# Fifteen slots for fetched expert rows, and one dot product in six on GpSimd and ScalarE, from the eighth top-k block on

## The chip, the cores and the metric

The kernel runs on one core of one Trainium2 chip. The metric is the device time of one execution in microseconds (us). The kernel before took 4034.56 us, the median of 3 runs (4030.64 to 4038.61).

## The reference, cut to what matters

One layer of a decoder trunk on 1024 tokens of width 1024: token mixers (a convolution and a stick-breaking attention), a cross-attention into 256 memory tokens, and then PEER, the retrieval of single-neuron experts, in which the change lies:

```
q = (h @ w_pq).reshape(b, s, 8, 2, 128)
sc = einsum('bshpc,pnc->bshpn', q, sub_keys)        # 128 keys on either side
top_v, top_i = top_k(sc, 16)
cand = top_v[..., 0, :, None] + top_v[..., 1, None, :]
best_v, best_i = top_k(cand, 16)
expert = i1 * 128 + i2                              # one of 16384
gate = softmax(best_v)
a = einsum('bthkd,btd->bthk', u_emb[expert], h)     # 16 experts of each of 8 heads
out = einsum('bthk,bthkd->btd', gelu(a) * gate, v_emb[expert])
```

The change concerns `a`, the dot products of the fetched rows of `u_emb` with the token's own `h`.

## The kernel before, in words

The kernel has four phases, one after the other: the mixers, the merge, `retrieve_phase` (L1406) and `spread_value_phase`. The tokens are treated in two halves of 512. For the first half (the "picked" half, 4 tiles of 128 tokens) the chosen experts' rows are fetched one by one and multiplied with `h` on the vector engine; for the second half (the "dense" half) TensorE multiplies `h` with all 16384 rows of `u_emb`, in 128 expert tiles.

**Top-k blocks.** `body(b)` (L2224) of the vector engine's program (DVE) finds the 16 best experts of one head for one half: `b` from 0 to 15, blocks 0 to 7 for the picked half and 8 to 15 for the dense one. It is a hand-written order of MAX8, FIND_INDEX8 and MATCH_REPLACE8 instructions and small table arithmetic. Between its steps stand `some(i)`, a sixteenth of the block's dot products each (`dots`, L2187), and `beside(b, at)` (L2200), which forms the low parts of weight tiles (`split_low`, L1380) for TensorE. There are 512 dot products, 8 heads x 4 token tiles x 16 experts, numbered `d`; `dots_before(b)` (L1512) shares them evenly over blocks 1 to 15, so that block 7 begins at d = 204.

**A dot product** (L2193) is one SCALAR_TENSOR_TENSOR on 128 partitions x 1024 elements. It reads the fetched rows in `slots[s]` and `h_rows[:, t]`, both in SBUF, writes the product back into the slot and sums it into `tables.coef`. It raises `dotted`.

**The fetches.** `fetch(d)` (L1575) is an indirect DMA issued by GpSimd (POOL): 128 rows of 4 KB, one for each partition, into slot `d % 7`. It waits until the dot product seven before it is done (`dotted`). The fetches are POOL's only work from the end of the cross-attention's output projection on; during that projection it also makes the low parts of eight weight tiles (`give_low`, L1585), three ahead of the first fetch and five between fetches.

**TensorE** (PE) runs `product` (L1385), 24 matmuls of 128x128 by 512 columns for each weight tile: high by high, high by low and low by high. The order of the tiles is fixed by `tile_order` (L1278): about nine expert tiles and the next head's two query tiles for each block. `hhi[0]` and `hlo[0]` are the high and low parts of the first half's `h`; their last reader is the tile ("query", 7, 1), whose place is after the third expert tile of block 6. **ScalarE** (ACT) makes a tile's high part (`split_high`, L1376), copies or gelus a product out of its PSUM bank (`query`, `expert`, L1922) and copies scores. The weights are loaded by the sync engine's queue (SP), one tile whenever the product four before it is done.

At the end of the phase ACT waits for all dot products and applies gelu to `coef` (L1950).

Of the kernel before, what the change touches and what calls it, by code (L numbers as in the profile page):

```python
# [14 lines left out]
P = 128  # L15
D = 1024
# [9 lines left out]
PH = 8  # L26
# [5 lines left out]
GT = 4  # L32
# [5 lines left out]
F32 = mybir.dt.float32  # L38
# [5 lines left out]
ALU = mybir.AluOpType  # L44
ACT = mybir.ActivationFunctionType
# [77 lines left out]
class SumSquares:  # L123
# [22 lines left out]
    def sum(self, nc, pe, ones):  # L146
        pe.wait_ge(self.added, NC)
        for h in range(2):
            mm = nc.tensor.matmul(self.out[:, h], ones, self.total[:, h * H:h * H + H], start=True, stop=True)
        mm.then_inc(self.done, 1)  # L150
# [1105 lines left out]
BLOCKS = 2 * PH  # L1256
# [1 line left out]
PICKED, DENSE = slice(0, TD), slice(TD, T)  # L1258
SIDE = (PICKED, DENSE)
EXPERT_LOADS = 4  # L1260
ROWS_SLOTS = 7
GELU_SLOTS = 5


# [141 lines left out]
def retrieve_phase(nc, carry, front, front_at, wide_at, room_at, weights, memory, tables, x_in, w_cross, w_query, u_stream, x_out, x2t, keysT, ffn_gain,  # L1406
# [8 lines left out]
    with Phase(nc, "ret") as m:  # L1415
# [28 lines left out]
        x_rows = [m.at(f"x_rows{t}", [P, D], F32, room_at + x * KB) for t, x in enumerate((83, 87, 91, 0))]  # L1444
        h_rows = m.at("h_rows", [P, GT, D], F32, room_at + 24 * KB)
        slots = [m.at(f"urow{s}", [P, D], F32, room_at + x * KB) for s, x in enumerate((53, 57, 61, 65, 69, 73, 0))]
        keys = m.at("keys", [P, 2, KEYS], F32, front_at + 4 * 8192)
        asked = [[xT[:, 3 + 2 * i + c, PICKED] for c in range(2)] for i in range(2)]
        bent_out = [xT[:, 3 + i, DENSE] for i in range(GELU_SLOTS)]
# [49 lines left out]
        gate_made = m.sem("gate_made", start=1)  # L1499
        held, slot_held = m.sem("held"), m.sem("slot_held")  # L1500
        rows_made = m.sem("rows_made")
        row_loaded = [m.sem(f"row_loaded{s}") for s in range(ROWS_SLOTS)]
        dotted = m.sem("dotted", start=ROWS_SLOTS)
        gelu_stored = [m.sem(f"gelu_stored{s}") for s in range(GELU_SLOTS)]
        turn_done, part_high, part_low = m.sem("turn_done"), m.sem("part_high"), m.sem("part_low")
        bent, coef_made = m.sem("bent"), m.sem("coef_made")
# [5 lines left out]
        def dots_before(b):  # L1512

            return DOTS * max(b - 1, 0) // (BLOCKS - 1)

        STARTS = [ORDER.index(("give", 1, 0)), ORDER.index(("give", 1, 2))] + [ORDER.index(("expert", 1, expert_at(b)))
                                                                                for b in range(FIRST_DENSE, BLOCKS)] + [len(ORDER) - 2]
# [47 lines left out]
        @block.gpsimd  # L1565
        def _(pool):
            nc.gpsimd.affine_select(out=ident[:], in_=ones[:], pattern=[[-1, P]], compare_op=ALU.is_equal, fill=0.0,
                                    base=0, channel_multiplier=1).then_inc(made, 1)
            for n, tile in enumerate(ORDER):
                if tiles.maker[n] and tile[:2] != ("give", 1):  # L1570
                    tiles.split_low(pool, nc.gpsimd, n)
            pool.wait_ge(h2_made, NC)
            nc.gpsimd.iota(place_at[:], pattern=[[KEYS, K]], base=0, channel_multiplier=0).then_inc(made, 1)
            nc.gpsimd.iota(fifteen[:].rearrange("p t k -> p (t k)"), pattern=[[0, ND * K]], base=K - 1, channel_multiplier=0).then_inc(made, 1)
            def fetch(d):  # L1575
                hd, k, s = d // (GT * K), d % (GT * K), d % ROWS_SLOTS
                t, j = k % GT, k // GT
                if k == 0:
                    pool.wait_ge(rows_made, hd + 1)
                pool.wait_ge(dotted, d + 1)  # L1580
                pool.sem_inc(slot_held, 1)
                nc.gpsimd.indirect_dma_start(slots[s][:], None, u_rows,  # L1582
                                             bass.IndirectOffsetOnAxis(tables.rows[:, t, hd * K + j:hd * K + j + 1], 0)).then_inc(row_loaded[s], 16)

            def give_low(k):  # L1585

                tiles.split_low(pool, nc.gpsimd, ORDER.index(("give", 1, k)))

            for k in range(3):
                give_low(k)  # L1590
            tile = ("weigh", 1, NC - 1)
            pool.wait_ge(banks.filled(tile), banks.turn(tile))
            pool.wait_ge(x2t_stored, 16 * GT)
            for d in range(DOTS):
                fetch(d)
                if d >= ROWS_SLOTS - 1 and (d - ROWS_SLOTS + 1) % 3 == 0 and (d - ROWS_SLOTS + 1) // 3 + 3 < NC:
                    give_low((d - ROWS_SLOTS + 1) // 3 + 3)

        @block.tensor
        def _(pe):  # L1600
# [162 lines left out]
        def _(act):  # L1763
# [117 lines left out]
            def query(b, c):  # L1881
                tile = ("query", b, c)
                act.wait_ge(banks.filled(tile), banks.turn(tile))
                if b >= 2:
                    act.wait_ge(scored, 2 * b - 2)
                nc.scalar.activation(asked[b % 2][c], banks.at(tile), ACT.Copy).then_inc(banks.emptied(tile), 1)
                ahead(tile)

            def copy_scores(b):
                for c in range(2):  # L1890
                    act.wait_ge(scored, 2 * b + c + 1)
                    act.wait_ge(index16, b * NU + 1)
                    if b == 0:
                        act.wait_ge(x2t_stored, 16 * GT)
                    nc.scalar.activation(sc[:, c], scps[:, c], ACT.Copy).then_inc(sc_made, 1)

            def exponent(b):
                act.wait_ge(shift_made, b + 1)
                nc.scalar.activation(expv[:], shifted[:], ACT.Exp).then_inc(exp_taken, 1)
# [22 lines left out]
            def expert(e):  # L1922
                tile = ("expert", 1, e)
                act.wait_ge(banks.filled(tile), banks.turn(tile))
                if e >= GELU_SLOTS:
                    act.wait_ge(gelu_stored[e % GELU_SLOTS], 16 * (e // GELU_SLOTS))
                nc.scalar.activation(bent_out[e % GELU_SLOTS], banks.at(tile), ACT.Gelu_apprx_tanh).then_inc(banks.emptied(tile), 1)
                ahead(tile)

            for b in range(FIRST_DENSE, BLOCKS):  # L1930
                for i, e in enumerate(experts_of(b)):
                    expert(e)
                    if i == 1:
                        exponent(b - 1)
                    if i == QUERY_BEHIND and b + 1 < BLOCKS:
                        for c in range(2):
                            query(b + 1, c)
                    if i == SCORES_BEHIND and b + 1 < BLOCKS:
                        copy_scores(b + 1)
            exponent(BLOCKS - 1)  # L1940

            def parts_high(r):
# [3 lines left out]

            for r in range(3):
                parts_high(r)
            act.wait_ge(dotted, DOTS + ROWS_SLOTS)
            nc.scalar.activation(tables.coef[:], tables.coef[:], ACT.Gelu_apprx_tanh).then_inc(bent, 1)  # L1950

        @block.vector
        def _(dve):
# [233 lines left out]
            def dots(d0, d1):  # L2187

                for d in range(d0, d1):
                    hd, k, s = d // (GT * K), d % (GT * K), d % ROWS_SLOTS  # L2190
                    t, j = k % GT, k // GT
                    dve.wait_ge(row_loaded[s], d // ROWS_SLOTS * 16 + 16)
                    nc.vector.scalar_tensor_tensor(out=slots[s][:], in0=slots[s][:], scalar=1.0, in1=h_rows[:, t], op0=ALU.mult, op1=ALU.mult,  # L2193
                                                   accum_out=tables.coef[:, t, hd * K + j:hd * K + j + 1]).then_inc(dotted, 1)

# [548 lines left out]
```

## Time and profile before

| | |
|---|---|
| median of 3 runs | 4034.56 us (4030.64 to 4038.61) |
| the profiled execution | 4050.63 us, its span 4048.8 us |
| granted TensorE clock, mean | 0.914 |
| busy | PE 3394.2, DVE 3201.9, POOL 1888.9, ACT 1457.9 us |
| top-k blocks 0 to 15 | 1661 to 2814 us of the span |
| of these, blocks 7 to 15 | 2158 to 2814 us |

Times in the trace count from the start of the span. A row of a group of instructions gives the busy time in all and the mean ns of one, and behind the bar how long the engine stood idle before them and what ended that. A row of the timeline gives start and duration in us; neighbouring instructions on one engine overlap by some 0.07 us in it, so that the distance of two starts is what an instruction costs in a full row. Where xN stands at its end, the row holds N instructions.

### The profile page before, as it was taken

What the parts mean: (1) busy time and instruction counts of PE and PEld (TensorE: products, weight loads), DVE (VectorE), ACT (ScalarE), POOL (GpSimd) and SP (SyncE); (2) the same over time, 40 slices, a digit from 0 to 9 for tenths busy, and PEclk for the clock granted to TensorE, in tenths of its full rate; (3) what the DMA queues carried; (4) which work ended last, traced back from release to release, by engine and by line L of the source; (5) the groups of instructions that cost most, each with busy time, mean ns of one, the idle gap of its engine ahead of it and who ended that gap; (6) DMA issues with size and microseconds to landing.
All of it is one profiled execution on the core that took longest, in us unless ns stands there. A gap on an engine that the chain in (4) does not pass through costs nothing. (4 is left out here: it accounts for less than half of the span.)

```text
span 4048.8 us, 46819 instructions
## 1 busy us (share of the span) xinstructions
PE 3394.2 (84%) x15298; PEld 2673.5 (66%) x15298; DVE 3201.9 (79%) x5528; ACT 1457.9 (36%) x2400; POOL 1888.9 (47%) x1508
## 2 busy tenths in 40 slices
PE   6999999998899998868989989897333788898886
PEld 5766676766577886646777777775333567677664
DVE  5677776777753513699999999998999798898988
ACT  3465555656542433222322322322222222222222
POOL 2433444333222131345556665554555466666664
PEclk9999999998999999979999999998555799999998
DMA  2111111111343322479999999997988999999997
GB/s 85 47 49 51 53 37 53 44 51 53 121 181 125 120 73 95 156 248 353 357 353 354 370 357 354 344 362 289 362 323 334 332 392 396 396 399 397 395 383 283
DMA packets 300338, 964.44 MB, mean 238 GB/s; under 512 B 30656, under 2 KB 63680, under 8 KB 297024
## 3 DMA queue, kind: packets, MB, share of 16 engines
q0 software_dynamic: 147456, 536.94, 35.3%
q1 hardware_dynamic: 150336, 390.95, 26.6%
q10 hardware_dynamic: 2304, 33.56, 2.1%
q8 instruction: 124, 2.03, 0.2%
q14 instruction: 118, 0.97, 0.1%
HBM read 861.18 MB, written 100.14 MB: 237 GB/s over the span
## 5 line engine op out<-in xcount | busy, mean ns | idle before, releaser
L2446 POOL DMA_INDIRECT spread_vrow<-in_v_rows,shared_pick_rows x512 | 712.5, 1392 | 464.9 <-DVE spread_y L2474 339.8
L1582 POOL DMA_INDIRECT ret_urow<-in_u_rows,shared_pick_rows x512 | 630.0, 1230 | 493.0 <-DVE ret_urow L2193 358.5
L2474 DVE SCALAR_TENSOR_TENSOR spread_y<-spread_vrow,shared_pick_coef,spread_y 128x1024 f32<-128x1024 f32 x512 | 639.3, 1279 | 10.1 <-DMA spread_vrow<-in_v_rows,shared_pick_rows 10.0
L2193 DVE SCALAR_TENSOR_TENSOR ret_urow<-ret_urow,ret_h_rows 128x1024 f32<-128x1024 f32 x512 | 609.8, 1227 | 28.7 <-DMA ret_urow<-in_u_rows,shared_pick_rows 26.5
L157 PE MATMUL shared_carry<-ret_hhi,shared_w_hi 128*128 128x512 f32 x1152 | 475.1, 412 | 108.6 <-DVE shared_w_lo L1382 66.1
L157 PE MATMUL spread_banks<-spread_ahi,spread_vhi 128*128 128x512 f32 x1024 | 418.8, 409 | 121.0 <-DVE spread_alo L2487 121.0
L157 PE MATMUL shared_carry<-shared_wide_hi,shared_w_hi 128*128 128x512 f32 x1152 | 459.1, 399 | 28.9 <-DVE shared_wide_lo L585 11.2
L158 PE MATMUL shared_carry<-ret_hlo,shared_w_hi 128*128 128x512 f32 x1152 | 466.0, 405 | 0.0
L158 PE MATMUL shared_carry<-shared_wide_lo,shared_w_hi 128*128 128x512 f32 x1152 | 454.8, 395 | 0.0
L159 PE MATMUL shared_carry<-shared_wide_hi,shared_w_lo 128*128 128x512 f32 x1152 | 454.2, 394 | 0.0
L158 PE MATMUL spread_banks<-spread_alo,spread_vhi 128*128 128x512 f32 x1024 | 412.1, 402 | 0.0
L159 PE MATMUL spread_banks<-spread_ahi,spread_vlo 128*128 128x512 f32 x1024 | 410.9, 401 | 0.0
L190 POOL TENSOR_TENSOR shared_w_lo<-shared_w_raw,shared_w_hi 128x1024 fp32r<-128x1024 f32 x78 | 203.5, 2611 | 390.2 <-ACT shared_w_hi L186 390.2
L157 PEld LDWEIGHTS shared_carry<-ret_hhi,shared_w_hi 128*128 128x128 f32 x1152 | 227.5, 197 | 173.3 <-issue 121.9
L636 DVE SCALAR_TENSOR_TENSOR shared_front<-mix_u,mix_cwj,shared_front 128x1024 f32<-128x1024 f32 x240 | 329.0, 1371 | 6.2 <-DVE mix_u L607 3.2
L157 PEld LDWEIGHTS spread_banks<-spread_ahi,spread_vhi 128*128 128x128 f32 x1024 | 200.4, 196 | 180.7 <-DVE spread_alo L2487 116.1
L159 PE MATMUL shared_carry<-ret_hhi,ret_wlow 128*128 128x512 f32 x768 | 311.8, 406 | 0.0
L159 PE MATMUL shared_carry<-ret_hhi,shared_w_lo 128*128 128x512 f32 x768 | 308.3, 401 | 0.0
L2582 PE MATMUL spread_banks<-spread_gate,spread_one 128*128 128x128 f16 x1024 | 113.9, 311 | 210.7 <-DVE spread_gate L2504 210.7
L2613 ACT ACTIVATE spread_ahi<-spread_act 128x512 fp32r<-128x512 f32 x128 | 81.0, 632 | 573.3 <-DVE spread_act L2483 573.3
L157 PEld LDWEIGHTS shared_carry<-shared_wide_hi,shared_w_hi 128*128 128x128 f32 x1152 | 219.7, 191 | 82.1 <-issue 28.2
L158 PEld LDWEIGHTS shared_carry<-ret_hlo,shared_w_hi 128*128 128x128 f32 x1152 | 228.0, 198 | 47.8 <-issue 1.0
(295 smaller groups left out, 6764.6 us busy)
## 6 DMA issues: line engine op xcount, KB each, us to landing
spread_vraw<-in_peer_v SPq DMA_DIRECT2D x128, 512.0 KB, 13.8
shared_w_raw<-in_peer_u SPq DMA_DIRECT2D x65, 512.0 KB, 7.1
gelu_u<-shared_front SPq DMA_DIRECT2D x128, 256.0 KB, 8.3
gates<-spread_stage ACTq DMA_DIRECT2D x16, 2048.0 KB, 9.6
spread_act<-gelu_u SPq DMA_DIRECT2D x128, 256.0 KB, 11.9
spread_graw<-gates SPq DMA_DIRECT2D x16, 2048.0 KB, 23.3
ret_wraw<-in_peer_u SPq DMA_DIRECT2D x63, 512.0 KB, 7.2
shared_w_raw<-in_w_mix SPq DMA_DIRECT2D x56, 512.0 KB, 3.4
```

The costliest lines, as they stand in the source:

```text
L157: nc.tensor.matmul(out, whi, xhi, start=(first and i == 0), stop=False)
L158: nc.tensor.matmul(out, whi, xlo, start=False, stop=False)
L159: mm = nc.tensor.matmul(out, wlo, xhi, start=False, stop=(last and i == len(terms) - 1))
L190: self.nc.gpsimd.tensor_tensor(self.lo[:, slot], self.raw[:, slot], self.hi[:, slot].bitcast(F32), ALU.subtract).then_inc(self.lo_made, 1)
L636: nc.vector.scalar_tensor_tensor(out=ybuf[:, par], in0=u[:, par, t:t + T], scalar=cwj[:, par, t:t + 1], in1=ybuf[:, par], op0=ALU.mult, op ...
L1582: nc.gpsimd.indirect_dma_start(slots[s][:], None, u_rows, bass.IndirectOffsetOnAxis(tables.rows[:, t, hd * K + j:hd * K + j + 1], 0)).then ...
L2193: nc.vector.scalar_tensor_tensor(out=slots[s][:], in0=slots[s][:], scalar=1.0, in1=h_rows[:, t], op0=ALU.mult, op1=ALU.mult, accum_out=tab ...
L2446: nc.gpsimd.indirect_dma_start(v_slots[s][:], None, v_rows, bass.IndirectOffsetOnAxis(tables.rows[:, t, j:j + 1], 0)).then_inc(row_loaded[ ...
L2474: nc.vector.scalar_tensor_tensor(out=y[:, t], in0=v_slots[s][:], scalar=tables.coef[:, t, j:j + 1], in1=y[:, t], op0=ALU.mult, op1=ALU.add ...
L2582: mm = nc.tensor.matmul(ps[:, bank, x], one1[:, b, t], gate[b][:, i, t], start=(i == 0), stop=(i == 1))
L2613: nc.scalar.activation(ahi[g % 2][:, e], act[:, e], ACT.Copy).then_inc(ahi_made, 1)
```

## The change

From dot 204 on (block 7, the eighth) the fetched rows go into fifteen slots: the seven of before and eight in the place of `hhi[0]` and `hlo[0]`. Before the fetch of dot 204 POOL waits for the tile ("query", 7, 1). Of the dots from 204 on each with d % 6 == 5 is no longer computed by DVE: POOL multiplies the slot with `h_rows` in place (TENSOR_TENSOR), behind the fetch six further on, and ACT sums the product by an ACTIVATE Copy with an accumulated output. `due` (of the ACT program) places these sums after the expert and query tiles, in proportion to the place of the tile in its block. Each fetch waits for whoever read its slot last, DVE or ACT.

```
@@ -1258,7 +1258,7 @@
-ROWS_SLOTS = 7
+ROWS_SLOTS, MORE_SLOTS = 7, 15
@@ -1444,6 +1444,7 @@
         slots = [m.at(f"urow{s}", [P, D], F32, room_at + x * KB) for s, x in enumerate((53, 57, 61, 65, 69, 73, 0))]
+        slots += [m.at(f"urow{ROWS_SLOTS + s}", [P, D], F32, wide_at + x * KB) for s, x in enumerate((0, 4, 8, 12, 32, 36, 40, 44))]
@@ -1499,8 +1500,8 @@
-        row_loaded = [m.sem(f"row_loaded{s}") for s in range(ROWS_SLOTS)]
-        dotted = m.sem("dotted", start=ROWS_SLOTS)
+        row_loaded = [m.sem(f"row_loaded{s}") for s in range(MORE_SLOTS)]
+        dotted, pool_dotted, pool_summed = m.sem("dotted"), m.sem("pool_dotted"), m.sem("pool_summed")
@@ -1512,6 +1513,17 @@
         def dots_before(b):
 
             return DOTS * max(b - 1, 0) // (BLOCKS - 1)
+
+        FIRST_POOLED, POOL_BEHIND = dots_before(PH - 1), 6
+        pooled = [d >= FIRST_POOLED and d % 6 == 5 for d in range(DOTS)]
+        slot_of = [d % ROWS_SLOTS if d < FIRST_POOLED else (d - FIRST_POOLED) % MORE_SLOTS for d in range(DOTS)]
+        held_by, landed, latest = [], [], {}
+        for d in range(DOTS):
+            user, loads = latest.get(slot_of[d], (None, 0))
+            held_by.append(user)
+            landed.append(16 * loads + 16)
+            latest[slot_of[d]] = d, loads + 1
+        upto = {kind: [sum(p is kind for p in pooled[:d]) for d in range(DOTS + 1)] for kind in (True, False)}
@@ -1573,12 +1585,17 @@
             def fetch(d):
-                hd, k, s = d // (GT * K), d % (GT * K), d % ROWS_SLOTS
+                hd, k, s = d // (GT * K), d % (GT * K), slot_of[d]
                 t, j = k % GT, k // GT
                 if k == 0:
                     pool.wait_ge(rows_made, hd + 1)
-                pool.wait_ge(dotted, d + 1)
-                pool.sem_inc(slot_held, 1)
+                if d == FIRST_POOLED:
+                    tile = ("query", PH - 1, 1)
+                    pool.wait_ge(banks.filled(tile), banks.turn(tile))
+                last = held_by[d]
+                if last is not None:
+                    pool.wait_ge(pool_summed if pooled[last] else dotted, upto[pooled[last]][last + 1])
+                    pool.sem_inc(slot_held, 1)
                 nc.gpsimd.indirect_dma_start(slots[s][:], None, u_rows,
                                              bass.IndirectOffsetOnAxis(tables.rows[:, t, hd * K + j:hd * K + j + 1], 0)).then_inc(row_loaded[s], 16)
 
@@ -1591,10 +1608,20 @@
             tile = ("weigh", 1, NC - 1)
             pool.wait_ge(banks.filled(tile), banks.turn(tile))
             pool.wait_ge(x2t_stored, 16 * GT)
+            def product(d):
+                s, t = slot_of[d], d % (GT * K) % GT
+                pool.wait_ge(row_loaded[s], landed[d])
+                nc.gpsimd.tensor_tensor(slots[s][:], slots[s][:], h_rows[:, t], ALU.mult).then_inc(pool_dotted, 1)
+
             for d in range(DOTS):
                 fetch(d)
+                if d >= POOL_BEHIND and pooled[d - POOL_BEHIND]:
+                    product(d - POOL_BEHIND)
                 if d >= ROWS_SLOTS - 1 and (d - ROWS_SLOTS + 1) % 3 == 0 and (d - ROWS_SLOTS + 1) // 3 + 3 < NC:
                     give_low((d - ROWS_SLOTS + 1) // 3 + 3)
+            for d in range(DOTS - POOL_BEHIND, DOTS):
+                if pooled[d]:
+                    product(d)
 
         @block.tensor
         def _(pe):
@@ -1927,16 +1954,39 @@
                 nc.scalar.activation(bent_out[e % GELU_SLOTS], banks.at(tile), ACT.Gelu_apprx_tanh).then_inc(banks.emptied(tile), 1)
                 ahead(tile)
 
+            summed_to = [0]
+
+            def sums(upto_dot):
+
+                for d in range(summed_to[0], max(upto_dot, summed_to[0])):
+                    if pooled[d]:
+                        hd, k, s = d // (GT * K), d % (GT * K), slot_of[d]
+                        t, j = k % GT, k // GT
+                        act.wait_ge(pool_dotted, upto[True][d + 1])
+                        nc.scalar.activation(slots[s][:], slots[s][:], ACT.Copy,
+                                             accum_out=tables.coef[:, t, hd * K + j:hd * K + j + 1]).then_inc(pool_summed, 1)
+                summed_to[0] = max(upto_dot, summed_to[0])
+
+            def due(tile):
+
+                n = tiles.place[tile]
+                b = max(b for b in range(FIRST_DENSE, BLOCKS) if STARTS[b] <= n)
+                first, after = dots_before(b), dots_before(b + 1)
+                return min(after, first + (after - first) * (n - STARTS[b]) // (STARTS[b + 1] - STARTS[b]))
+
             for b in range(FIRST_DENSE, BLOCKS):
                 for i, e in enumerate(experts_of(b)):
                     expert(e)
+                    sums(due(("expert", 1, e)))
                     if i == 1:
                         exponent(b - 1)
                     if i == QUERY_BEHIND and b + 1 < BLOCKS:
                         for c in range(2):
                             query(b + 1, c)
+                            sums(due(("query", b + 1, c)))
                     if i == SCORES_BEHIND and b + 1 < BLOCKS:
                         copy_scores(b + 1)
+            sums(DOTS)
             exponent(BLOCKS - 1)
 
             def parts_high(r):
@@ -1946,7 +1996,8 @@
 
             for r in range(3):
                 parts_high(r)
-            act.wait_ge(dotted, DOTS + ROWS_SLOTS)
+            act.wait_ge(dotted, upto[False][DOTS])
+            act.wait_ge(pool_summed, upto[True][DOTS])
             nc.scalar.activation(tables.coef[:], tables.coef[:], ACT.Gelu_apprx_tanh).then_inc(bent, 1)
 
         @block.vector
@@ -2187,9 +2238,11 @@
             def dots(d0, d1):
 
                 for d in range(d0, d1):
-                    hd, k, s = d // (GT * K), d % (GT * K), d % ROWS_SLOTS
+                    if pooled[d]:
+                        continue
+                    hd, k, s = d // (GT * K), d % (GT * K), slot_of[d]
                     t, j = k % GT, k // GT
-                    dve.wait_ge(row_loaded[s], d // ROWS_SLOTS * 16 + 16)
+                    dve.wait_ge(row_loaded[s], landed[d])
                     nc.vector.scalar_tensor_tensor(out=slots[s][:], in0=slots[s][:], scalar=1.0, in1=h_rows[:, t], op0=ALU.mult, op1=ALU.mult,
                                                    accum_out=tables.coef[:, t, hd * K + j:hd * K + j + 1]).then_inc(dotted, 1)
 
```

## Rows read from the trace of the kernel before

**Rows 1.** The page: GB/s in 40 equal slices of the span.

```profile
GB/s 85 47 49 51 53 37 53 44 51 53 121 181 125 120 73 95 156 248 353 357 353 354 370 357 354 344 362 289 362 323 334 332 392 396 396 399 397 395 383 283
```

**Rows 2.** Busy time by stretch: block 7, and blocks 7 to 15.

```profile
2158.40:2229.81 71.41, 66.68 (x286) 54.23 (x285) 70.81 (x201) 21.54 (x28) 46.07 (x36) 0.95 0.97 360
...
2158.40:2814.50 656.10, 586.13 (x2479) 475.55 (x2478) 636.39 (x1795) 190.69 (x238) 383.02 (x304) 0.94 0.96 355
```

The columns are the stretch, its length, then busy us and instructions of PE, PEld, DVE, ACT and POOL, the granted clock, the DMA share and GB/s.

**Rows 3.** Waits in blocks 7 to 15: who waited for whom, us, times, longest.

```profile
DVE ret_urow L2193 <- DMA ret_urow<-in_u_rows,shared_pick_rows: 12.7, 17, 2.0
...
PE shared_carry L157 <- DVE ret_wlow L1382: 42.6, 17, 5.2
...
POOL ret_urow L1582 <- DVE ret_urow L2193: 193.7, 85, 5.6
```

**Rows 4.** Groups of DVE instructions in blocks 7 to 14 (2158.40 to 2744.14).

```profile
L2193 DVE SCALAR_TENSOR_TENSOR ret_urow<-ret_urow,ret_h_rows 128x1024 f32<-128x1024 f32 x273 | 322.2, 1217 | 12.7 <-DMA ret_urow<-in_u_rows,shared_pick_rows 11.5
L1382 DVE TENSOR_TENSOR shared_w_lo<-ret_wraw,shared_w_hi 128x1024 fp32r<-128x1024 f32 x44 | 53.9, 1225 | 0.0
L1382 DVE TENSOR_TENSOR ret_wlow<-shared_w_raw,shared_w_lo 128x1024 fp32r<-128x1024 f32 x23 | 28.0, 1219 | 1.6 <-ACT shared_w_lo L1378 1.6
L1382 DVE TENSOR_TENSOR ret_wlow<-shared_w_raw,shared_w_hi 128x1024 fp32r<-128x1024 f32 x22 | 26.9, 1223 | 0.2 <-ACT shared_w_hi L1378 0.2
```

**Rows 5.** Timeline of DVE where block 7 begins.

```profile
2155.26 1.22 DVE L2193 SCALAR_TENSOR_TENSOR ret_urow<-ret_urow,ret_h_rows 128x1024 f32<-128x1024 f32 x1
...
2162.28 1.22 DVE L2193 SCALAR_TENSOR_TENSOR ret_urow<-ret_urow,ret_h_rows 128x1024 f32<-128x1024 f32 x1
...
2163.42 1.22 DVE L2193 SCALAR_TENSOR_TENSOR ret_urow<-ret_urow,ret_h_rows 128x1024 f32<-128x1024 f32 x1
```

**Rows 6.** Timeline of POOL in block 1: its elementwise instructions between fetches.

```profile
1693.80 2.35 POOL L1382 TENSOR_TENSOR ret_wlow<-shared_w_raw,shared_w_lo 128x1024 fp32r<-128x1024 f32 x1
...
1700.59 2.40 POOL L1382 TENSOR_TENSOR shared_w_lo<-ret_wraw,shared_w_hi 128x1024 fp32r<-128x1024 f32 x1
...
1707.42 2.38 POOL L1382 TENSOR_TENSOR shared_w_lo<-ret_wraw,shared_w_hi 128x1024 fp32r<-128x1024 f32 x1
...
1716.41 2.35 POOL L1382 TENSOR_TENSOR ret_wlow<-shared_w_raw,shared_w_hi 128x1024 fp32r<-128x1024 f32 x1
...
1723.49 2.60 POOL L1382 TENSOR_TENSOR ret_wlow<-shared_w_raw,shared_w_lo 128x1024 fp32r<-128x1024 f32 x1
```

**Rows 7.** Timeline of DVE beside them.

```profile
1694.80 0.28 DVE L2099 MATCH_REPLACE8 ret_sc<-ret_top,ret_sc 128x128 f32<-128x128 f32 x1
1695.22 2.03 DVE L2193 SCALAR_TENSOR_TENSOR ret_urow<-ret_urow,ret_h_rows 128x1024 f32<-128x1024 f32 x1
...
1698.93 0.68 DVE L2028 TENSOR_TENSOR shared_front<-shared_front,ret_sq 128x512 f32<-128x512 f32 x1
...
1701.08 3.00 DVE L2193 SCALAR_TENSOR_TENSOR ret_urow<-ret_urow,ret_h_rows 128x1024 f32<-128x1024 f32 x1
...
1707.26 3.63 DVE L2193 SCALAR_TENSOR_TENSOR ret_urow<-ret_urow,ret_h_rows 128x1024 f32<-128x1024 f32 x1
...
1715.51 3.48 DVE L2111 TENSOR_TENSOR ret_cand<-ret_top 128x64 f32<-128x64 f32 x4
...
1724.35 2.29 DVE L2028 TENSOR_TENSOR shared_front<-shared_front,ret_sq 128x512 f32<-128x512 f32 x1
...
2183.11 0.62 DVE L2111 TENSOR_TENSOR ret_cand<-ret_top 128x64 f32<-128x64 f32 x4
```

**Rows 8.** POOL's fetches: blocks 7 to 14 as a group, and landings of blocks 7 to 15.

```profile
L1582 POOL DMA_INDIRECT ret_urow<-in_u_rows,shared_pick_rows x275 | 350.0, 1273 | 238.3 <-DVE ret_urow L2193 174.6 <-issue 63.7
...
DMA to landing us min/median/max: 4.4/8.2/12.9
```

**Rows 9.** Timeline of POOL: one fetch of the slow form.

```profile
2156.45 1.99 POOL L1582 DMA_INDIRECT ret_urow<-in_u_rows,shared_pick_rows  x1 [0.30 <-issue]
```

**Rows 10.** ACT instructions of L2648: a sum over 1024 elements, as the change adds.

```profile
L2648 ACT ACTIVATE spread_vrow<-spread_y x4: 1040/1040/1057, 4013.6 to 4016.7; 128x1024 f32<-128x1024 f32 x4
```

## The prediction

> **What bounds the kernel now.** I read the stretches by block first, because the change touches only blocks 7 to 15. There DVE is busy for 636.4 of 656.1 us, 97%, and in block 7 for 70.8 of 71.4 us, while POOL is busy for 383 us, ACT for 191 us and PE for 586 us [rows 2]. The waits come next. DVE waits 12.7 us for fetched rows in the whole stretch, PE waits for low parts that DVE makes (42.6 us for one of the two tiles alone), and POOL waits 193.7 us for DVE to release slots [rows 3]. So everybody waits for DVE, and DVE for almost nobody. The end of the stretch is set by the sum of DVE's instructions; deeper slots have 12.7 us to gain, and only time taken off DVE has more. The DMA share of 0.96 at 355 GB/s [rows 2] looks like a second bound, to which I come below.
>
> **The dots taken from DVE.** Dots 209, 215, ..., 509 go, which is (509 - 209)/6 + 1 = 51 of the 308 from 204 on. In a full row a dot costs the distance of two starts, 1.14 us [rows 5]. That is 51 x 1.14 = 58.1 us off DVE.
>
> **What the product on POOL costs DVE.** The kernel before already has such a meeting: in block 1 POOL runs five elementwise instructions of 128x1024 of 2.35 to 2.60 us between fetches, while DVE runs the same dots [rows 6, 7]. Put beside each other:
> - POOL from 1693.80 to 1696.15. DVE's MATCH_REPLACE8 at 1694.80 takes its usual 0.28 us; the dot that starts at 1695.22 takes 2.03 us, not 1.22: 0.81 us more, and ends 1.10 us after POOL does.
> - POOL from 1700.59 to 1702.99. The dot at 1701.08 takes 3.00 us: 1.78 more. Again it ends 1.09 us after POOL.
> - POOL from 1707.42 to 1709.80. The dot at 1707.26 takes 3.63 us: 2.41 more, POOL's whole duration.
> - POOL at 1716.41: the four small additions of L2111 take 3.48 us where they take 0.62 elsewhere, 2.86 more. POOL at 1723.49: an addition of L2028 takes 2.29 us, not 0.68, 1.61 more.
>
> The dots are not slowed, they stand still until POOL is through. The mean of the five is (0.81 + 1.78 + 2.41 + 2.86 + 1.61)/5 = 1.89 us. The size depends on what DVE has at hand: instructions with two operands in SBUF stop, the searches with one go on. Dots and low parts, at 1.14 us each, fill (273 + 44 + 23 + 22) x 1.14 = 413 of the 585.7 us of blocks 7 to 14 [rows 4], so at least 71% of DVE's time is of the kind that stops. 0.71 x 2.39 = 1.70 us is then a lower estimate and the full 2.39 us an upper one. I take 1.89, the measured mean of the nearest rows, which lies between: 51 x 1.89 = 96.4 us on DVE. The ends for the range are the mean of the three smallest, (0.81 + 1.61 + 1.78)/3 = 1.40, and the full 2.39 us: 71 and 122 us.
>
> The Trainium skill has a rule on this (SBUF — State Buffer, section "SBUF: two separate sides"): the port pair that VectorE and GpSimd share is an exclusive lock for a whole instruction, and a VectorE instruction with two SBUF inputs needs it against a GpSimd instruction that reads SBUF. Applied without a discount for one-input work it charges the whole of each product, 51 x 2.39 = 122 us, which would put the result at about 4092; the rows say that a part falls on searches that go on.
>
> **The slots.** Up to 12.7 us of DVE's waits for rows [rows 3] can go. A row lands 8.2 us after its issue at the median and 12.9 at most [rows 8]; a dot passes every 656.1/308 = 2.13 us [rows 2], so seven slots cover 15 us less the issue and fifteen cover 32. I take 11 us off; the ends are 0 and 12.7. The change of slots costs once: dot 204 goes into slot 0, where 203 was, not 197, so its fetch can only start when dot 203 is done. In the trace that is at 2156.4, and dot 204 starts at 2162.28, 5.9 us on [rows 5]. The fetch takes about 1.3 us on POOL and 8.2 us to land [rows 8], 9.5 in all, so DVE waits 3.6 us; I take 4, between 0 and 8. The wait for the tile ("query", 7, 1) costs nothing: that tile stands behind the third expert tile of block 6, and block 6 is over when dot 204 is due.
>
> **POOL.** It issues as many fetches as before, 34.1 a block at 1273 ns + 0.30 us of issue [rows 8, 9], 53.7 us, and 5.7 products of 2.39 us plus up to 0.6 us for the DVE instruction in flight, 17 us. The sum is 71 us in a block of now some 77; it fits, with 6 us to spare. Behind a product only fetches are queued, and fifteen slots hide a delay of 3 us.
>
> **ACT.** 51 sums of 1.04 us [rows 10], some 55 to 65 us with the reading of the sum, beside 191 us in 656 [rows 2]. It stands behind the making of the next high part, in time in which ACT waits for PE, so I cost it at nothing; if that cover went, it would be at most about 1.2 us for each. ACT waits for POOL there, with its gelus and high parts queued behind. The product is asked for when dot d - 9 is done, nine dots or 19 us ahead of DVE's own place, and ACT asks at about DVE's place; it finds it done. PE waits for DVE already; it waits more.
>
> **The sum.** -58.1 + 96.4 - 11 + 4 = +31 us. Against the profiled execution, 4050.6 becomes 4082; it lies 16 us above the median of the runs, so for the median 4034.6 + 31 = 4066 us. What a measurement can tell here from no change is 0.2%, 8 us.
>
> **The rivals.**
> - *POOL and DVE run beside each other* (faster). If the products fell on searches, or a multiplication did not stop the dots, the change would be worth -58.1 - 11 + 4 = -65 us, about 3970. A part of that comes with a share of overlap: it decides where the mean stop per product is under (58.1 + 7 - 8)/51 = 1.12 us. Only one of the five meetings is below that [rows 7]: 8%. The DMA engines would not forbid it: the stretch would need 355 x 656/591 = 394 GB/s, and slices of the next phase reach 396 to 399 [rows 1]. The same page of the Trainium skill gives some 358 GB/s as the limit between HBM and one core, by which the DMA would hold this rival at no gain at all; the trace disagrees, by those slices.
> - *The stop and the saving cancel* (same): a mean stop of about 1.3 us, if the products follow the release of a slot by DVE and so tend to meet the table work. 51 x 1.3 = 66, -58 - 7: +1 us, about 4036. 5%.
> - *POOL becomes the bound* (slower still). A fetch takes 1.99 us where a DVE instruction has just begun [rows 9], and behind a product DVE always has one waiting. If the mean rose from 1.27 to 1.7 us, a block would take POOL 34.1 x 2.0 + 17 = 85 us against 77, 8 more in each of nine blocks: +31 + 72, about 4137. It decides from a mean of 1.45 us on. Against it: 1273 ns is the mean under the same crowd of dots. 5%.
> - *The whole product stops DVE* (2.39 us each and no wait saved): 122 - 58 + 4 = +68, 4102; the upper end of the forecast, not a case of its own.
>
> **How the numbers follow.** The forecast, DVE bound with a stop of 1.4 to 2.4 us, has 82%: its own range goes from 71 - 58 - 12.7 + 4 = +4, which is 4039, to 4102. The range of 8 in 10 leaves out the gain, POOL as the bound and the very ends: 4042 to 4094. Faster by over 0.2%: 8%. Within 0.2%: the 5% and a sliver of the forecast's lower end, 6%. Slower: 86%.
>
> **What the changed profile would show.** Right: dots of L2193 beside a POOL TENSOR_TENSOR of 2 to 3.6 us, 51 of them or nearly, and a mean of that group of up to 1.22 + 96/257 = 1.6 us, less what falls on other instructions; the blocks from 7 on at 76 to 78 us instead of 73; DVE waits for rows of a few us, one of 4 us at the start of block 7; POOL's products at 2.4 to 3.4 us; PE's waits for low parts up by about 30 us. Wrong: dots that stay at 1.22 us beside the products; ACT waiting for POOL with PE behind it; POOL without idle time. The forecast falls if the mean stop is under 1.3 us, or if DVE has idle time again in the stretch.

## The result, and the profile after

The changed kernel takes 4076.5 us (median of 4 runs, 4071.9 to 4080.5), the kernel before 4036.6 us (4 runs beside it): a ratio of 1.010, 95% interval 1.0081 to 1.0118. It is 40 us slower; the forecast was 31. Beside the experiments the kernel before took 4033 to 4035 us (medians of 17 to 23 runs); by these the loss is 41 to 44 us. The profiled execution took 4071.9 us, its span 4070.2 us.

Busy time by stretch in the changed kernel, columns as in [rows 2]: block 7, and blocks 7 to 15.

```profile
2146.99:2226.15 79.16, 67.55 (x285) 54.69 (x284) 75.18 (x191) 25.84 (x36) 67.62 (x46) 0.94 0.98 358
...
2146.99:2830.30 683.31, 593.40 (x2465) 480.31 (x2464) 674.85 (x1692) 240.12 (x337) 559.68 (x359) 0.92 0.95 343
```

The stretch is 27 us longer than in [rows 2] (29 us from the first search of block 7 to the start of the last dot), and DVE's busy time grew by 38 us although 51 dots have gone. POOL's went from 383 to 560 us. DVE is still the engine with hardly any idle time. Its groups in blocks 7 to 14 (2146.99 to 2758.07) answer to [rows 4]:

```profile
L2246 DVE SCALAR_TENSOR_TENSOR ret_urow<-ret_urow,ret_h_rows 128x1024 f32<-128x1024 f32 x228 | 326.4, 1464 | 4.6 <-DMA ret_urow<-in_u_rows,shared_pick_rows 3.4
L1382 DVE TENSOR_TENSOR shared_w_lo<-ret_wraw,shared_w_hi 128x1024 fp32r<-128x1024 f32 x44 | 60.1, 1366 | 0.0
L1382 DVE TENSOR_TENSOR ret_wlow<-shared_w_raw,shared_w_lo 128x1024 fp32r<-128x1024 f32 x23 | 32.5, 1413 | 0.0
```

228 dots now take as long as 273 did: 1464 ns each instead of 1217. The low parts of the weights, which the change does not touch, went from 1225 and 1219 to 1366 and 1413 ns. One meeting, in the timelines of POOL and of DVE:

```profile
2343.03 2.57 POOL L1614 TENSOR_TENSOR ret_urow<-ret_urow,ret_h_rows 128x1024 f32<-128x1024 f32 x1
```

```profile
2342.13 1.22 DVE L2246 SCALAR_TENSOR_TENSOR ret_urow<-ret_urow,ret_h_rows 128x1024 f32<-128x1024 f32 x1
...
2343.27 3.40 DVE L1382 TENSOR_TENSOR ret_wlow<-shared_w_raw,shared_w_hi 128x1024 fp32r<-128x1024 f32 x1
```

POOL's product ends at 2345.60. DVE's instruction, due after 1.22 us, ends at 2346.67, 1.07 us behind it, the picture of [rows 7]. Going through all 51 products in the trace: 45 of them stopped a DVE instruction for 1 us or more (28 dots, 8 low parts and 9 instructions of the small table arithmetic), and six lay beside searches and stopped nothing. What DVE's instructions took beside the products beyond the median of their kind is 101 us, 1.98 us for each product, from 0.01 to 2.89. The waits in blocks 7 to 15 answer to [rows 3]:

```profile
DVE ret_urow L2246 <- DMA ret_urow<-in_u_rows,shared_pick_rows: 3.4, 3, 1.5
...
PE shared_carry L157 <- DVE ret_wlow L1382: 48.5, 17, 6.2
...
POOL ret_urow L1599 <- DVE ret_urow L2246: 28.2, 15, 10.0
POOL ret_urow L1599 <- ACT ret_urow L1966: 13.6, 8, 4.8
```

DVE waits 3.4 us for rows, ACT does not wait for POOL at all, and POOL waits 28 us for DVE where it waited 194. PE's waits for low parts, which DVE makes, are 90 us in both kinds of tile together; they were 70.

### The profile page after: what moved, and what is told of

Its sections match the earlier page's. It is cut to its first block and busy times, and to the rows that moved or that the text cites. A ratio compares the mean times of both kernels' runs of the same rounds, so it can differ in the third digit from the quotient of the medians.

```text
span 4070.2 us, 46855 instructions
## 1 busy us (share of the span) xinstructions
PE 3405.1 (84%) x15298; PEld 2679.8 (66%) x15298; DVE 3241.3 (80%) x5426; ACT 1509.1 (37%) x2502; POOL 2062.5 (51%) x1559
## 5 line engine op out<-in xcount | busy, mean ns | idle before, releaser
L1599 POOL DMA_INDIRECT ret_urow<-in_u_rows,shared_pick_rows x512 | 678.1, 1324 | 328.5 <-DVE ret_urow L2246 170.0
L1954 ACT ACTIVATE shared_front<-shared_carry 128x512 f32<-128x512 f32 x128 | 76.5, 598 | 493.0 <-PE shared_carry L159 493.0
```

The lines of the kernel that those rows point to most:

```text
L1599: nc.gpsimd.indirect_dma_start(slots[s][:], None, u_rows, bass.IndirectOffsetOnAxis(tables.rows[:, t, hd * K + j:hd * K + j + 1], 0)).then ...
```

## The experiments

Three theories: (A) a product on POOL stops DVE's instructions with two SBUF operands until it is over, (B) the loss lies in the slots, (C) it lies in POOL's occupation or ACT's sums. The kernel before ran beside all of them, at medians of 4033 to 4035 us. Times of "blocks 7 to 15" are from the first search of block 7 to the start of the last dot in the profile.

**The slots alone.**

```
-        pooled = [d >= FIRST_POOLED and d % 6 == 5 for d in range(DOTS)]
+        pooled = [False for d in range(DOTS)]
```

> The fifteen slots alone: DVE keeps all 512 dots, POOL and ACT get none. Theory A (a product on POOL stops every DVE instruction with two SBUF operands until it is over, and nothing else costs): without products only the slots are left, 4036.6 - 11 (waits for rows) + 4 (the fetch of dot 204 behind dot 203), about 4030 us, 4022 to 4036. Theory B (the loss of the change lies in the slots or in the place of the eight new ones): 4050 or more.

Measured: 4029.9 us (12 runs), ratio 0.9991 (0.9981 to 1.0000). B falls: the slots gain some 3 us, if anything. DVE's waits for rows are 1.0 us in the stretch, and blocks 7 to 15 last 637 us against the changed kernel's 682. The products and sums thus cost 4076.5 - 4029.9 = 47 us, with 58 us of dots gone: (47 + 58)/51 = 2.05 us for each product; by the profiles (45 + 58)/51 = 2.02. By DVE's busy time alone, 674.9 us against 631.7 - 58.1, it is 1.98.

**Without the product.** DVE leaves out its 51 dots, ACT sums the rows as they are, POOL does not multiply.

```
-                nc.gpsimd.tensor_tensor(slots[s][:], slots[s][:], h_rows[:, t], ALU.mult).then_inc(pool_dotted, 1)
+                pool.sem_inc(pool_dotted, 1)
```

> The 51 multiplications on POOL are left out; DVE still leaves out its 51 dots and ACT sums the rows as fetched, so 51 coefficients are sums of rows, not dot products. Theory A: DVE has 58 us less and no stop, 4036.6 - 58 - 11 + 4, about 3972 us, unless TensorE or the DMA engines take over as the bound (then up to 3990); all dots at 1.22 us. Theory C (POOL's occupation or ACT's sums and their waits are what costs): ACT's part would still be there, so not under 4025 if it is ACT; if it is POOL's occupation, as theory A.

Measured: 3980.3 us, ratio 0.987 (0.9855 to 0.9889). So 96 us of the changed kernel's time hang on the 51 multiplications, 1.9 us on each. That is a little less than the stops themselves, for with them gone DVE meets other waits: 4.2 us for rows and 7.5 us for the high parts that ACT makes, 12 us against 3.4 in the changed kernel. With these 8 us the price is 2.05 us, and they would account for the 8 us between the measured 3980 us and the 3972 of theory A. ACT's sums, which are still there, cost at most these few us. DVE's dots in this stretch are back at their old duration, and the DMA engines carry 396 GB/s over nearly 600 us (stretch of blocks 7 to 15, columns as before):

```profile
2151.39:2743.10 591.71, 559.36 (x2475) 459.03 (x2474) 574.68 (x1690) 242.80 (x338) 416.00 (x308) 0.98 1.01 396
```

**Writes in place of the product.** POOL is as busy, or more, but reads nothing; 51 coefficients are 0.

```
-                nc.gpsimd.tensor_tensor(slots[s][:], slots[s][:], h_rows[:, t], ALU.mult).then_inc(pool_dotted, 1)
+                for part in range(3):
+                    nc.gpsimd.memset(slots[s][:], 0.0).then_inc(wiped, 1)
+                    pool.wait_ge(wiped, 3 * upto[True][d] + part + 1)
+                pool.sem_inc(pool_dotted, 1)
```

> In place of each multiplication POOL writes zeros over the slot three times, one after the other, about 1 us each; the 51 coefficients are 0. It is busy for 3 us in each place, longer than with the product, but reads nothing from SBUF. Theory A in the form that only a GpSimd instruction that reads SBUF stops DVE: as without the product, 3972 to 3990 us, dots at 1.22 us. Theory A in the form that any GpSimd access stops DVE: 4076 to 4110 us, dots of 2 us and more beside the writes. Theory C (POOL's occupation delays the fetches): 4076 us or more, dots at 1.22 us, and DVE waiting for rows.

Measured: 4063.0 us, ratio 1.008 (1.0056 to 1.0108). Of the times expected none was met: 4063 lies far above the 3972 to 3990 of reads alone and a little under the 4076 of the other two. The rows tell them apart. The dots of blocks 7 to 15 (min/median/max), and who DVE waited for there:

```profile
L2250 DVE SCALAR_TENSOR_TENSOR ret_urow<-ret_urow,ret_h_rows x257: 1198/1221/1279, 2162.2 to 2821.1; 128x1024 f32<-128x1024 f32 x129
```

```profile
DVE ret_urow L2250 <- DMA ret_urow<-in_u_rows,shared_pick_rows: 69.8, 54, 5.1
```

Of the 257 dots 81 ran beside one of the 153 writes of 0.96 us, and none was stopped: the longest took 1.28 us. Nor was any low part, at most 1.29 us. So an instruction of this kind is stopped by a product and not by a write. It does not hold for every DVE instruction: at three places small TENSOR_SCALAR instructions, with one SBUF operand, stood still until a write was over. At one of them four in a row take 1.17 us, where they take 0.49 in another block; they end 0.21 us behind the last of POOL's three writes:

```profile
2435.80 1.17 DVE L2196 TENSOR_SCALAR ret_shift<-ret_bidx 128x64 uint32<-128x64 uint32 x4
```

```profile
2433.76 3.00 POOL L1616 MEMSET ret_urow<- 128x1024 f32 x3
```

The three places add 2 to 3 us in all, too little to explain 4063. But DVE stood 70 us waiting for rows, for POOL had become the bound. Its timeline, one group of three writes and the fetch behind it:

```profile
2314.14 3.00 POOL L1616 MEMSET ret_urow<- 128x1024 f32 x3
2318.05 0.94 POOL L1600 DMA_INDIRECT ret_urow<-in_u_rows,shared_pick_rows  x1 [0.90 <-POOL ret_urow L1616]
```

The group with its waits takes 3.9 us, so a block takes POOL 34.1 x 1.56 + 5.7 x 3.9 = 75 us, and the blocks last 70 to 77 us. So POOL's occupation is a second bound behind A, in this kernel, where POOL is busy for longer than with the product. In the changed kernel DVE waits 3.4 us for rows, so there it is not what costs.

**The product twice.** The product is repeated in place, so 51 coefficients carry h squared.

```
+                nc.gpsimd.tensor_tensor(slots[s][:], slots[s][:], h_rows[:, t], ALU.mult).then_inc(wiped, 1)
+                pool.wait_ge(wiped, upto[True][d + 1])
                 nc.gpsimd.tensor_tensor(slots[s][:], slots[s][:], h_rows[:, t], ALU.mult).then_inc(pool_dotted, 1)
```

> Each of POOL's 51 multiplications is done twice in a row, so that 51 coefficients carry h squared. Theory A: 51 more stops of 1.9 us, 4076.5 + 97, about 4173 us, 4150 to 4200. Theory C with POOL's fetches as what costs: POOL would need 73 + 15 us for each block of then 88, so a like time, but with DVE's waits for rows in the tens of us and not under 15 us. If the change's loss had another cause than the product: within 10 us of 4076.

Measured: 4184.8 us, ratio 1.038 (1.0361 to 1.0403). 108 us for 51 more products, 2.1 us each; the dots' mean rises to 1628 ns:

```profile
L2249 DVE SCALAR_TENSOR_TENSOR ret_urow<-ret_urow,ret_h_rows 128x1024 f32<-128x1024 f32 x257 | 411.0, 1628 | 22.2 <-DMA ret_urow<-in_u_rows,shared_pick_rows 20.8
```

DVE's waits for rows, 21 us, lie between the under 15 of theory A and the tens of us of theory C: POOL is near its limit too. What decides is DVE's busy time in blocks 7 to 15. It grew from 675 to 773 us, 98 us or 1.92 us for each added product, and the waits for rows grew by 17.

**The kernel before, once more.** No edit, one execution.

> The kernel before once more, for a second profile. The profile on which the prediction rests took 4050.6 us where the median is 4034; theory: its DVE waited more for fetched rows than usual, 12.7 us in blocks 7 to 15. In a run near the median those waits are a few us, and blocks 7 to 15 take about 645 us rather than 656. Rival: the difference lies elsewhere, and these blocks take 656 us again.

Measured: 4034.6 us. Blocks 7 to 15 last 644 us against 653 in the first profile, and DVE waits 5.7 us for rows there, not 12.7. The execution that the prediction's profile shows lay 16 us above the median of the kernel, and part of the slack in it was no property of the kernel. Against this second profile the changed kernel's blocks are 38 us longer (682 against 644), which fits the 40 us of the times.

**The slots without the drain**, that is, without the fetch of dot 204 having to wait until dot 203 has left the same slot.

```
-        slot_of = [... (d - FIRST_POOLED) % MORE_SLOTS for d in range(DOTS)]
+        slot_of = [... (d - FIRST_POOLED + 1) % MORE_SLOTS for d in range(DOTS)]
```

> The fifteen slots alone, numbered so that dot 204 goes into slot 1, where 197 was, not into slot 0 behind dot 203. Theory: 4 us of DVE waiting at the start of block 7 go, about 4026 us against 4030 of the slots alone. Rival: the wait at that place is hidden, 4030.

Measured (again without products): 4027.3 us (11 runs), ratio 0.998 (0.9969 to 0.999). That is 2.6 us less than the slots alone; the intervals overlap, so the two values expected, 4026 and 4030, are not told apart. In the changed kernel dot 204 waited 1.5 us.

**h in PSUM for every fourth dot** of the changed kernel.

```
+            nc.scalar.activation(h_last, h_rows[:, GT - 1], ACT.Copy).then_inc(h_last_made, 1)
...
-  ... in1=h_rows[:, t], ...
+  ... in1=h_last if t == GT - 1 else h_rows[:, t], ...
```

> The changed kernel, but the h rows of the fourth token tile are copied once into two PSUM banks that lie idle then, and every fourth dot of DVE reads h from there: one operand in SBUF, one in PSUM. Theory A: such a dot is never stopped, 1.2 to 1.3 us beside a product too. DVE has one quarter fewer dots that can stop, so the stop is shorter by some 0.3 us on average: 51 x 0.3 = 15 us, 4060 us, 4050 to 4068. Rival: the product stops every DVE instruction of this kind, wherever its second operand lies: 4076, and dots of the fourth tile of 2 to 4 us as well. A price for reading PSUM would show in their duration.

Measured: 4060.3 us, ratio 1.007 (1.0054 to 1.0087), 16 us under the changed kernel. All dots of the run, by where their second operand lies:

```profile
L2253 DVE SCALAR_TENSOR_TENSOR ret_urow<-ret_urow,ret_h_rows x358: 1196/1217/4081, 1685.8 to 2811.6; 128x1024 f32<-128x1024 f32 x179
...
L2253 DVE SCALAR_TENSOR_TENSOR ret_urow<-ret_urow,ret_side x103: 1195/1211/1222, 1692.5 to 2812.7; 128x1024 f32<-128x1024 f32 x103
```

Ten of the 103 dots with h in PSUM ran beside a product; none took more than 1.22 us. With both operands in SBUF it was up to 4.08. One product with a dot of either kind beside it:

```profile
2377.99 2.44 POOL L1616 TENSOR_TENSOR ret_urow<-ret_urow,ret_h_rows 128x1024 f32<-128x1024 f32 x1
```

```profile
2378.96 1.21 DVE L2253 SCALAR_TENSOR_TENSOR ret_urow<-ret_urow,ret_side 128x1024 f32<-128x1024 f32 x1
...
2380.09 1.42 DVE L2253 SCALAR_TENSOR_TENSOR ret_urow<-ret_urow,ret_h_rows 128x1024 f32<-128x1024 f32 x1
```

The first lies wholly inside the product and is not stopped. The second starts 0.34 us before the product's end, at 2380.43, and ends 1.08 us behind it. Reading h from PSUM costs nothing here. The 16 us came as forecast and by the forecast's way: the stops add up to 85 us, not 101.

**Products beside searches.** Products wait for a signal of DVE, given ahead of a run of searches. P is the block's first dot, and a pair (a, b) in MEETINGS says that POOL, behind fetch P + a, waits for the signal and then multiplies dot P + b. The slots are numbered as in the run without the drain.

```
+MEETINGS = ((12, 5), (14, 8), (18, 14))
+        PLAN = [(dots_before(b) + at, dots_before(b) + d) for b in range(PH, BLOCKS) for at, d in MEETINGS]
...
+                for n, (at, of) in enumerate(PLAN):
+                    if at == d:
+                        pool.wait_ge(searching, n + 1)
+                        product(of)
...
+                dve.sem_inc(searching, 1)
                 first_best()
```

> Only 24 dots go to POOL and ACT, three in each of blocks 8 to 15, and each product waits for a signal that DVE gives just before a run of searches with one SBUF operand (ahead of first_best, of the second find_and_cut, and of find_second). Slots numbered as in the run without drain. Theory A: the product lies beside searches that it does not stop, the first wholly (3.9 us of searches against 2.4), the other two but for some 0.4 us: 24 x 1.14 = 27 us off DVE, 16 x 0.4 = 6 on it, so 21 us under the slots alone, about 4006 us, 3998 to 4014; dots longer than 2 us nearly vanish. Rival: POOL comes too late or DVE cannot be kept clear of it, stops of 2.0 us as before: 24 x 0.86 = 21 us above the slots alone, 4050.

Measured: 4028.4 us, ratio 0.9987 (0.9975 to 0.9999). Neither value: 16 of the 24 products still stopped a dot, because POOL came late. It never stood waiting for the signal, which had been given each time when it got there. The mean stop was 1.33 us, between the theory's and the rival's.

**The same, POOL at its place earlier,** `MEETINGS = ((8, 5), (11, 8), (15, 11))`, without and with the h of the fourth tile in PSUM.

> The aligned kernel came late: in its trace POOL reached the wait for DVE's signal some 4 us after the searches had begun, behind late fetches, and 16 of 24 products stopped a dot. Here POOL comes to the waits after fetch P + 8, P + 11 and P + 15 (P the block's first dot; before P + 12, P + 14, P + 18), so that it stands there ahead of DVE, and multiplies dots P + 5, P + 8 and P + 11. Theory A: dots beside a product mostly at 1.22 us, the blocks from 8 on at 68 to 69 us instead of 71 to 72, 24 x 1.14 - 8 x 0.8 = 21 us under the slots without drain (4027), about 4006 us, 3999 to 4014. Rival: the products meet dots all the same, or POOL's waiting makes rows late: 4022 to 4035.

> The same, with the h rows of the fourth token tile read from PSUM by DVE's dots. Theory A: where a product outlasts its searches, one dot in four is not stopped; little is left to save, 0 to 5 us under the run with the earlier waits alone, about 4003 us. Rival, as there: 4018 to 4030, some 5 us less than that run.

Measured: 4039.0 us (ratio 1.0009, 0.9999 to 1.0018) and 4024.8 us (0.9978, 0.9967 to 0.999). The forecasts of 4006 and 4003 failed; 20 dots were stopped in the first kernel and 14 in the second. The wait moved: POOL, ahead of DVE in its program, stood waiting for the rows it was to multiply, for 17.6 us in the first and 21.2 in the second. Its timeline in the first shows why it had fetched them so late:

```profile
2431.40 1.97 POOL L1601 DMA_INDIRECT ret_urow<-in_u_rows,shared_pick_rows  x1 [0.30 <-issue]
2433.68 1.99 POOL L1601 DMA_INDIRECT ret_urow<-in_u_rows,shared_pick_rows  x1 [0.30 <-issue]
```

In a row of dots a fetch begins every 2.28 us, the length of two dots. A fetch too stands behind a DVE instruction with two SBUF operands that has just begun, and POOL falls into DVE's beat. The run with h in PSUM for every fourth dot shows that the operands decide: the 16 fetches that begin within 0.15 us of the start of a dot with h in PSUM take 0.93 to 0.98 us, the 40 that begin so in a dot with both operands in SBUF 1.98 at the median. At 2.28 us for a fetch POOL does not gain on a DVE that needs one every 2.1; over all of blocks 7 to 15, where the mean fetch takes 1.47 us and 0.30 between two, it does keep up but for 5.0 us of DVE's waits for rows.

The second kernel is 14 us faster than the first, where 0 to 5 was expected. In the profiles, 11 us apart, it has 5 us less of stops and none of the 5.0 us of waits for rows; no run tells why these waits went.

**Two products a block, of rows long landed,** `MEETINGS = ((7, 3), (10, 6))`, with and without h in PSUM.

> In the last two kernels POOL's fetches kept the beat of DVE's dots, one fetch in two dots, so that POOL was only some eight dots ahead and then waited 18 to 21 us for the very rows that it was to multiply; most products met dots. Here POOL takes only two dots in each of blocks 8 to 15, P + 3 and P + 6, whose rows have landed, behind fetch P + 7 and P + 10, ahead of first_best and of the second find_and_cut, and the h rows of the fourth tile lie in PSUM. Theory A: 16 x 1.14 = 18 us off DVE, about 8 x 0.6 = 5 us of stops: 13 us under the slots without drain (4027), 4014, 4008 to 4019; DVE waits for rows under 5 us. Rival: POOL has no time for products at all in this beat, and they meet dots or make rows late: 4022 or more.

> The same with h in SBUF for all tiles. Theory A: the second product of a block outlasts its searches and stops a dot for up to 0.8 us each time; with the fourth tile in PSUM one in four of those is free, so this one is 0 to 5 us above that, about 4016. Rival: 4025 or more.

Measured: 4027.0 us (0.9983, 0.9969 to 0.9997) and 4020.5 us (0.9971, 0.996 to 0.9983). The first forecast, 4014, failed: its time is that of the rival, for seven of its 16 products still stopped a dot, and the stops came to 16 us where 5 were expected. The second lies between its forecast of 4016 and the rival's 4025. It has the lowest median of the kernels here that compute all dot products, 14 us under the kernel before. Its 7 us under the slots without the drain are not settled by the times, whose intervals overlap; in the profiles its blocks 7 to 15 last 627 us against 636. A meeting that works, POOL and then DVE:

```profile
2373.67 2.42 POOL L1616 TENSOR_TENSOR ret_urow<-ret_urow,ret_h_rows 128x1024 f32<-128x1024 f32 x1
```

```profile
2373.36 1.64 DVE L2146 MAX8 ret_top<-ret_sc 128x8 f32<-128x128 f32 x8
...
2377.25 1.21 DVE L2247 SCALAR_TENSOR_TENSOR ret_urow<-ret_urow,ret_h_rows 128x1024 f32<-128x1024 f32 x1
```

The product lies wholly beside searches and the dot behind them takes its 1.21 us. Five of its 16 products stopped something (four dots and one low part), for 0.97 to 2.25 us, where in the changed kernel 45 of 51 did. That the version with PSUM is not better than the one without was not expected; their intervals overlap, and it stays open.

**What the stops add up to.** For each kernel with products, read from its profile: the products, the mean stop of one, all stops, the dots taken off DVE at 1.14 us, DVE's waits for rows, the sum of these three, and by how much blocks 7 to 15 are in fact longer than the 636.4 us of the slots without the drain. All in us.

| kernel | products | mean stop | stops | dots | waits | sum | measured |
|---|---|---|---|---|---|---|---|
| product twice | 102 | 1.92 | +196 | -58 | +21 | +159 | +161 |
| changed kernel | 51 | 1.98 | +101 | -58 | +3 | +46 | +46 |
| changed, h in PSUM | 51 | 1.67 | +85 | -58 | +3 | +30 | +28 |
| beside searches | 24 | 1.33 | +32 | -27 | 0 | +5 | +6 |
| earlier | 24 | 1.30 | +31 | -27 | +5 | +9 | +9 |
| earlier, h in PSUM | 24 | 1.11 | +27 | -27 | 0 | 0 | -2 |
| two landed, h in PSUM | 16 | 0.99 | +16 | -18 | 0 | -2 | -3 |
| two landed | 16 | 0.59 | +9 | -18 | 0 | -9 | -9 |

So the failed forecasts failed in where the products fell, not in what a stop costs.

## Why the prediction was right

**The bound and the direction held.** DVE bounded the stretch before and after, and a product on POOL costs it more than a dot saves. Forecast and measured agree by mechanism: the stops are there, on dots, low parts and table arithmetic, and vanish on dots and low parts without the product and with writes in its place, and on dots whose second operand lies in PSUM.

**The stop** was put at 1.89 us from five meetings; it is 1.98 by DVE's instructions (2.02 by the length of the blocks, 2.05 by the medians, 1.9 to 2.05 from the run without the product). The share of a product that DVE stands still was right: 1.89/2.39 is 0.79, and 1.98/2.52 is 0.79. Too small was the product, which takes 2.52 us on average in the changed kernel, not 2.39. That five meetings between 0.81 and 2.86 us gave the mean of 51 between 0.01 and 2.89 so closely is luck in part. "The full 2.39 us an upper one" held for the mean, not for a single stop. The share of DVE's time put at "at least 71%" is 413/585.7 = 70.5%, which changes nothing in the forecast.

**The slots** were the term that was off: "Up to 12.7 us of DVE's waits for rows can go" came from one profile 16 us above its median; a second one shows 5.7 us. The slots with their drain give 3 us by the medians against the forecast's 7. The drain itself was 1.5 us, not 4.

**The sum.** Stops of 101 instead of 96.4 us and slots of -3 instead of -7 make +31 into +40, which is what the four runs beside the kernel before gave.

**The signs in the profile.** Blocks 7 to 14 take 74 to 79 us, 76 on average, where 76 to 78 was said; POOL's products 2.35 to 2.87 us (2.4 to 3.4); PE's waits for low parts rose by 20 us (30). "51 of them or nearly" was too many dots: 28 were stopped for 1 us or more, since 8 low parts and 9 pieces of table arithmetic took their share.

**POOL** was said to fit "with 6 us to spare". With fetches at 1.40 us on average in the stretch, not 1.27, and products at 2.5, it takes 34.1 x 1.70 + 5.7 x 2.7 = 73 us of a block of 76: 3 us to spare (an estimate from these means).

**The rival that POOL and DVE run side by side**, at 3970 us, was wrong in its price, not only in its chance. The run with writes is a side by side that stops no dot, and it took 4063 us. With a product of 2.5 us in place of 3.9 POOL would need about 53 + 15 = 68 us for a block (an estimate from its rows), against 71 with the slots alone: such a change would have gained some 25 to 30 us on the slots alone, not 58. That is not shown: in no run did reading products leave all of DVE's dots alone, and h in PSUM for all four tiles was not tried. The DMA engines, which that rival also named, were no bar: 396 GB/s in the run without the product.

**ACT** costs next to nothing, as forecast. It holds slots a little longer, 13.6 us of POOL's waits, while DVE waits only 3.4 us for rows.

## What to carry to other kernels

Work moved from VectorE to GpSimd is not work taken off VectorE when both read SBUF: before counting the saving, find a place in the trace where the two already meet and read how long VectorE's instruction grows. Here the mean stop went from 1.98 us, for products put anywhere, to 0.59 for products put beside searches, and only under the 1.14 us of a dot does the move pay. For that GpSimd must have its data early, since its own DMA issues lose time to VectorE too. The gain left was small: the best such kernel is 0.3% under the kernel before, and how much of that is more than the deeper slots give is not settled. And read the slack from two profiles, not from one whose time lies above the median.

## What was not expected of the hardware

- GpSimd writing SBUF (MEMSET of 128x1024, 0.96 us) does not stop a SCALAR_TENSOR_TENSOR or TENSOR_TENSOR of 128x1024 with two SBUF operands: at most 1.28 us in 257 dots, 81 of them beside a write. A GpSimd TENSOR_TENSOR, which reads, does: up to 4.08 us for 1.22. But a TENSOR_SCALAR with one SBUF operand can be stopped by the writes too: four in a row took 1.17 us for 0.49.
- MAX8, FIND_INDEX8 and MATCH_REPLACE8 are stopped by neither: 121 of them ran beside a product in the run with the product twice and 139 beside a write, and none took over 0.02 us more than the median of its kind.
- GpSimd's indirect DMA issue, 0.94 us alone, takes 1.97 to 1.99 us when a VectorE instruction with two SBUF operands has just begun, and settles into a beat of 2.28 us beside dots of 1.14 us. In a dot with one operand in PSUM it takes 0.93 to 0.98 us.
- A SCALAR_TENSOR_TENSOR of 128x1024 is as fast with an operand in PSUM (1211 ns at the median) as with both in SBUF (1217 ns), and ten of them beside products stayed at 1.22 us or less.
